# Every second column for the weight loads, and reversed streams, in sixteen column chunks of a two-block transformer kernel

## The chip, the cores and the metric

The kernel runs on one core of a Trainium2 chip. The metric is device time in microseconds (us) of that core. TensorE (PE in the profile) multiplies; VectorE (DVE) and ScalarE (ACT) prepare its operands and take its results away; the DMA queue of SyncE (SPq) brings the weights from HBM. GpSimd does nothing here.

## The reference

Two transformer blocks on one sequence of 256 tokens and 2048 features, in float32. The first block is a gated linear recurrence beside dilated attention. What matters for the change is its input projection `w_in` and what is done with two of its column ranges, `rnn_gate` and `g_rnn`, 2048 columns each:

```python
h = rms_norm(x, ln_pre_g[layer])
proj = jnp.einsum('bsd,de->bse', h, w_in[layer])
rnn_x, rnn_gate, q, k, v, attn_gate, g_rnn, g_attn = split_columns(proj)
hr = rg_lru(rnn_x, ...)                                  # convolution, two gates, a scan over time
y_rnn = jnp.einsum('bsc,cd->bsd', hr * jax.nn.silu(rnn_gate), w_rnn_out[layer])
...                                                      # three groups of dilated attention -> y_attn
merged = jax.nn.sigmoid(g_rnn) * y_rnn + jax.nn.sigmoid(g_attn) * y_attn
y = jnp.einsum('bsd,de->bse', merged, w_o[layer])
x = x + rms_norm(y, ln_post_g[layer])
```

The second block does two layers of three attention branches, each with a wide input projection, a branch projection and an output projection. The change does not touch its arithmetic.

## The kernel before

**Precision.** Every weight and every activation is held as a pair of fp32r numbers, high and low: `hi` is the number copied into fp32r, `lo` is the rest. A product is `hi*hi + hi*lo + lo*hi`. Activations stand transposed, features on the partitions: `hT` (and `uT`) holds for each of 16 feature tiles 512 columns, 256 tokens of `hi` and then 256 of `lo`.

**A unit** is 1024 rows by 256 columns of a weight matrix, 8 row tiles of 128. Its two halves `h` = 0, 1 have 4 row tiles each. The DMA brings a half into `raw` (L390), ScalarE copies it to `hi` in `hl` (L945), VectorE writes `lo = raw - hi` into `hl` (L1288), and TensorE multiplies. `j` (0 or 1) says which half of the 2048 rows of the matrix a unit is and which of the two slots of `hl` it lies in. Two units, `j` = 0 and 1, make a chunk `c` of 256 output columns, in two PSUM banks of `pg` (`s` = 0, 1, 128 columns each).

**A pair** is what TensorE does for one row tile `k` and one bank `s`: a *wide* matmul, with the 128x128 `hi` weights loaded and all 512 columns of `hT` streamed, and a *narrow* one, with the `lo` weights loaded and the 256 columns of `hi` of `hT` streamed into the second half of the bank. So a pair is two weight loads of 128 columns and 768 streamed columns; a half unit is 4 row tiles x 2 banks = 8 pairs, 16 matmuls. The weights of bank `s` are the columns `s*128` to `s*128+127` of the row tile's 256, side by side in `hl`.

**The values of the attention** take the form `token_major`: there the activations are loaded and the weights streamed, `hi` and `lo` in one pattern of 2 x 256. A pair has the same two loads and 768 columns.

**Order.** It is written out by hand in the source. TensorE waits for `lo_done` before each half, and before the first half of a chunk for `evac_done` (its banks are free). `in_order` sets the order of wide and narrow inside a half: wide and narrow in turn, but for the row tiles listed in the table `SIDE`, where the wide ones of both banks come first and then the narrow ones.

**Where the change is.** Stage RG: 16 chunks, of which 0 to 7 are `rnn_gate` and 8 to 15 are `g_rnn`; 16 chunks x 2 units x 2 halves = 64 halves, 512 pairs, all on `hT`. Between chunks TensorE also computes the gates of the recurrence (L716: 64 matmuls of 256 columns on plain fp32 operands of `xres` into `pa`), while ScalarE and VectorE work on the recurrence beside their splitting of weights. The layout of `hl` is used by all stages: `part(j, e, h, a, n)` (L226) gives the place of slot `j`, `hi` or `lo` (`e`), half `h`.

Of the kernel before, what the change touches and what calls it, by code (L numbers as in the profile page):

```python
# [22 lines left out]
P = 128  # L23
S = 256
D = 2048
NT = D // P
UC = 2048
CH = 256
NCH = D // CH
# [6 lines left out]
RNN_X, RNN_G, QKV, D_QKV = 0, 2048, 4096, 3072  # L36
Q1, K1, V1 = QKV, QKV + D_QKV, QKV + 2 * D_QKV
Z1 = QKV + 3 * D_QKV
G_RNN, G_ATT = Z1 + 1024, Z1 + 1024 + D
# [54 lines left out]
def ends(first, last):  # L94

    return frozenset(range(first)) | frozenset(range(8 - last, 8))
# [6 lines left out]
SIDE = {  # L103
    "RX": {4: AGAIN},
    "RG": {3: ends(0, 1), 4: ends(1, 0), 7: ends(0, 1), 8: ends(1, 0), 11: ends(0, 1), 12: ends(1, 0), 15: ends(0, 1),
           16: ends(1, 0), 21: ends(0, 1), 22: AGAIN, 23: ends(0, 1), 24: AGAIN},
    "1": {15: ends(0, 2), 16: ends(1, 0), 17: ends(0, 1), 18: ALL, 19: ends(1, 0), 20: ends(0, 1), 21: ends(1, 1),
          22: ends(2, 0)},
    "B": {4: ends(0, 2), 5: ends(2, 0), 6: ends(0, 2), 7: ends(1, 0), 8: ends(0, 1), 9: ends(2, 2), 10: ALL, 11: ends(6, 0)},
    "C": {4: ends(0, 2), 5: ends(2, 0), 6: ends(0, 2), 7: ends(1, 0), 8: ends(0, 1), 9: ends(2, 2), 10: ends(1, 1),  # L110
          11: ends(4, 0)},
# [25 lines left out]
U_RX, U_RG, U_GR, U_YR, U_P1 = 0, 16, 32, 48, 64  # L137
C_RX, C_RG, C_GR, C_YR, C_P1 = 0, 8, 16, 24, 32
# [17 lines left out]
RAW_CHUNKS, RAW_HEAD = 5, 6  # L156


HI_AT, LO_AT, SLOT, HL = 16, UC + 32, 2 * UC + 128, 4 * UC + 224


PRE_SUMS = [1, 2 + NCH, 4 + 2 * NCH]
# [33 lines left out]
def build(nc, xT, w_in, w_gate, w_rnn, w_att, w_o, w_in2, w_uq, w_ukv, w_br, w_out2,  # L196
          vec1, vec2, blam, consts, tabs, bias_c, outT):
    ctx = ExitStack()
    with ctx:
# [25 lines left out]

        def part(j, e, h, a=0, n=UC // 2):  # L226

            first = j % 2 * SLOT + (LO_AT if e else HI_AT) + h * UC // 2 + a
            return hl[:, first:first + n]

        h3 = hT[:, :].rearrange("p (t n) -> p t n", n=512)
# [5 lines left out]
        pg3 = pg[:, :].rearrange("p (b n) -> p b n", n=512)  # L237
# [71 lines left out]
        block = ctx.enter_context(nc.Block())  # L309
# [232 lines left out]
        def _(pe):  # L542
            def mm(out, lhsT, rhs, start, stop):
                return nc.tensor.matmul(out, lhsT, rhs, start=start, stop=stop, skip_group_check=True)  # L544

            def split_view(j, n):

                return [[part(j, e, k * n // (UC // 2), k * n % (UC // 2), n) for k in range(UC // n)] for e in range(2)]

            def in_order(ks, subs, side, wide, narrow):  # L550

                if RUNS in side and len(ks) == 4 and ks[0] % 8 == 0:
                    for k in ks:
                        for s in range(subs):
                            wide(k, s)
                    for k in ks:
                        for s in range(subs):
                            ins = narrow(k, s)
                    return ins
                for k in ks:  # L560
                    for s in range(subs):
                        wide(k, s)
                        if k % 8 not in side:
                            ins = narrow(k, s)
                    if k % 8 in side:
                        for s in range(subs):
                            ins = narrow(k, s)
                return ins

            def feature_major(b, subs, wh, wl, op, ks, start, stop, base, side):  # L570

                return in_order(
                    ks, subs, side,
                    lambda k, s: mm(pg3[:, b + s, :], wh[k - base][:, s * P:s * P + P], op[:, k, :], start and k == ks[0], False),
                    lambda k, s: mm(pg3[:, b + s, S:], wl[k - base][:, s * P:s * P + P], op[:, k, 0:S], False,
                                    stop and k == ks[-1]))

            def token_major(b, hiw, both, op, ks, start, stop, base, side):

                return in_order(  # L580
                    ks, 2, side,
                    lambda k, s: mm(pg3[:, b + s, :], op[:, k, s * P:s * P + P], both[k - base], start and k == ks[0], False),
                    lambda k, s: mm(pg3[:, b + s, S:], op[:, k, S + s * P:S + s * P + P], hiw[k - base], False,
                                    stop and k == ks[-1]))

            def apart_view(j, n):

                return [[part(j, e, h, 0, n) for h in range(2)] for e in range(2)]

            def both_view(j, n):  # L590
                views = []
                for k in range(UC // n):
                    h, a = k * n // (UC // 2), k * n % (UC // 2)
                    first = j % 2 * SLOT + HI_AT
                    pair = hl[:, first:first + 2 * (LO_AT - HI_AT)].rearrange("p (e n) -> p e n", e=2)
                    views.append(pair[:, :, h * UC // 2 + a:h * UC // 2 + a + n])
                return views

            def opening(u0, c0, tiles_ready, first_parts, weights_parts=None, summed=None):
# [20 lines left out]
            def unit(u, j, c, cj, op, first, last, form="f", subs=2, ready=None, halves=(0, 1), first_parts=None, side=()):  # L620

                base = 0 if first else 8
                if form == "k":
                    base, first, last = 0, True, True
                wh, wl = split_view(j, CH)
                if form == "r":
                    wh, wl = ([[w[h][:, k * P:k * P + P] for k in range(4)] for h in range(2)] for w in apart_view(j, 512))
                for h in halves:
                    pe.wait_ge(lo_done, 2 * u + h + 5)
                    if first and h == 0 and c is not None:  # L630
                        pe.wait_ge(evac_done, c + 1)
                    start, stop = first and h == 0, last and h == 1
                    parts = [range(base + 4 * h, base + 4 * h + 4)] if form != "k" or h == 0 else [(4, 5), (6, 7)]
                    if first_parts is not None and h == 0:
                        parts = first_parts
                    for n, ks in enumerate(parts):
                        if ready is not None:
                            ready(ks)
                        b, begin, end = 2 * (cj % 2), start and n == 0, stop and n == len(parts) - 1
                        if form == "r":  # L640
                            ins = feature_major(b, subs, wh[h], wl[h], op, ks, begin, end, base + 4 * h, side)
                        elif form == "t":
                            ins = token_major(b, wh, both_view(j, CH), op, ks, begin, end, base, side)
                        else:
                            ins = feature_major(b, subs, wh, wl, op, ks, begin, end, base, side)
                    ins.then_inc(half_done, 1)
# [60 lines left out]
            def recurrence_gates(q):  # L707
                pe.wait_ge(rc_conv, q + 1)
                pe.wait_ge(rw_landed, 32 * (q // 2 + 1))
                for k in range(4):  # L710
                    t = 4 * (q % 2) + k
                    if q:
                        pe.wait_ge(rc_sig, 4 * q + k - 3)
                    for j in range(2):
                        w = xres[:, (8 + 4 * j) * S:(12 + 4 * j) * S]
                        ins = nc.tensor.matmul(pa3[:, k, j * S:j * S + S], w[:, t * P:t * P + P], x3[:, t, :],  # L716
                                               start=True, stop=True, skip_group_check=True)
                    ins.then_inc(rc_mm, 1)
# [6 lines left out]
            for c in range(2, NCH):  # L725
                for j in range(2):
                    unit(U_RX + 2 * c + j, j, C_RX + c, c, u3 if c < RAW_CHUNKS else h3, j == 0, j == 1,
                         ready=(lambda ks: h_split(0)(ks[0] // 4)) if c == RAW_CHUNKS else None,
                         side=SIDE["RX"].get(2 * c + j, ()))
            for c in range(2 * NCH):  # L730
                for j in range(2):
                    unit(U_RG + 2 * c + j, j, C_RG + c, c, h3, j == 0, j == 1, side=SIDE["RG"].get(2 * c + j, ()))
                for _, q in rec_pe[c]:
                    recurrence_gates(q)
            product(U_YR, C_YR, u3, lambda q: pe.wait_ge(ru_ready, 1 + q))
# [164 lines left out]
            for l in range(2):  # L900
                ul, cl_ = U_L + l * LU_N, C_L + l * LC_N
                for c in range(8):
# [5 lines left out]
                    for j in range(2):  # L908
                        for halves in ((0,), (1,)):
# [5 lines left out]
                                 side=SIDE["head"][l].get(2 * c + j, ()))  # L915
# [5 lines left out]
                for kind in "ABC":  # L921
                    turns = 2 if kind == "A" else 1
                    with pe.Fori(0, PAIRS // turns) as i:
                        for n in range(turns):
                            p = i * turns + n
# [8 lines left out]
        def _(act):  # L934
# [87 lines left out]

            def recurrence(step, q):
                r, i, _, mq = rec(q)
                if step == "tap":
                    xc = rec(q)[2]
# [933 lines left out]
```

## Time and profile before

| | |
|---|---|
| Median of 2 runs | 3123.56 us (3123.31 to 3123.81) |
| The profiled execution: own time | 3123.54 us |
| its span, first to last instruction | 3121.6 us |
| TensorE busy | 3100.0 us (99%) |
| TensorE weight loads busy (beside the matmuls) | 2732.4 us (88%) |
| VectorE busy | 2129.6 us (68%) |
| ScalarE busy | 1734.3 us (56%) |
| DMA share, mean rate | 59.3% of 16 engines, 183 GB/s |
| Granted TensorE clock, mean | 0.998 of 2.4 GHz |
| Stage RG in the span | 99.06 to 288.84 us |

Busy time of TensorE runs from a matmul's start to its modelled end, and matmuls overlap (a wide one is shown with 391 ns, though the next starts well before). What one costs must be read as the distance from start to start: a stretch divided by the matmuls that start in it. The span is 1.9 us short of the execution's own time; this part is taken as fixed.

### The profile page before, as it was taken

Reading aid. Unit: us, or ns where it says so; the run is one execution under the profiler, and the core shown is the slowest. Engines: PE = TensorE matmul, PEld = TensorE weight load, DVE = VectorE, ACT = ScalarE, POOL = GpSimd, SP = SyncE. Lnnn points to the kernel's source line nnn. Section 1 sums busy time; section 2 is a strip of 40 time slices with the busy share of each in tenths; the row PEclk is TensorE's granted clock in tenths of the full one; section 3 lists DMA queues with packets and bytes.
Section 4 is the critical chain, followed back from the end, with each engine's and each line's share of the span. In section 5 each row is a group of like instructions: output and inputs, shape, how many; then the busy total and the mean of one; then the engine's idle time right before and its main releaser. Section 6 shows DMA issues by size and latency. Waiting matters only on the chain.

```text
span 3121.6 us, 52176 instructions
## 1 busy us (share of the span) xinstructions
PE 3100.0 (99%) x18230; PEld 2732.4 (88%) x18230; DVE 2129.6 (68%) x2741; ACT 1734.3 (56%) x2291; POOL 0.2 (0%) x4
## 2 busy tenths in 40 slices
PE   8999999999999899999999999999999999999999
PEld 7888888888888789888888888888888888888888
DVE  7677575766667687766766656777776676665675
ACT  5685444444445556656565555645665656555563
POOL 0000000000000000000000000000000000000000
PEclk9999999999999999999999999999999999999999
DMA  7656665555556565565556666566556555665555
GB/s 230 197 171 202 200 190 169 187 180 172 179 174 211 174 176 159 158 203 173 177 172 194 189 182 182 183 205 185 159 158 203 173 177 172 194 189 183 181 183 180
DMA packets 569809, 571.67 MB, mean 183 GB/s; under 512 B 26352, under 2 KB 565488, under 8 KB 569712
## 3 DMA queue, kind: packets, MB, share of 16 engines
q1 hardware_dynamic: 569712, 570.42, 59.3%
q8 instruction: 56, 0.92, 0.1%
q14 instruction: 41, 0.34, 0.0%
HBM read 568.25 MB, written 2.10 MB: 183 GB/s over the span
## 4 chain that ended last, share of the span: by engine, by line
PE 98%; DVE 1%; ACT 1%; issue 0%; DMA 0%; SPq 0%; ACTq 0%; DVEq 0%
PE pg L544 92%; PE pa L783 1%; PE pa L800 1%; PE pa L544 1%; PE pa L790 1%; PE pa L759 1%; PE pa L801 1%; PE pa L716 0%; DVE hl L1288 0%; PE pa L890 0%; DMA raw<-w_in 0%; ACT hl L945 0%; DVE uT L1369 0%; DVE xres L1747 0%; PE pa L739 0%
## 5 line engine op out<-in xcount | busy, mean ns | idle before, releaser
L544 PE MATMUL pg<-hT,hl 128*128 128x512 f32 x11456 | 2003.8, 335 | 0.9 <-DVE hl L1288 0.9
L544 PEld LDWEIGHTS pg<-hT,hl 128*128 128x128 f32 x11456 | 1742.6, 188 | 241.8 <-DVE hl L1288 4.6
L1288 DVE TENSOR_TENSOR hl<-raw,hl 128x1024 fp32r<-128x1024 f32 (+1 forms) x1071 | 1255.6, 1209 | 304.5 <-ACT hl L945 296.2
L945 ACT ACTIVATE hl<-raw 128x1024 fp32r<-128x1024 f32 (+1 forms) x1071 | 1085.4, 1044 | 300.9 <-PE pg L544 278.9
L544 PE MATMUL pg<-uT,hl 128*128 128x256 f32 (+1 forms) x3712 | 631.4, 331 | 16.9 <-DVE uT L1369 7.9
L544 PEld LDWEIGHTS pg<-uT,hl 128*128 128x128 f32 x3712 | 555.7, 189 | 88.4 <-issue 14.8
L953 ACT ACTIVATE corr<-pg 128x512 f32<-128x512 f32 x286 | 170.3, 595 | 820.8 <-PE pg L544 820.8
L544 PE MATMUL pg<-hl,hT 128*128 128x256 f32 (+1 forms) x1792 | 318.7, 337 | 0.0
L544 PEld LDWEIGHTS pg<-hl,hT 128*128 128x128 f32 x1792 | 276.3, 188 | 39.7
L1295 DVE TENSOR_TENSOR work<-pg,corr 128x512 f32<-128x512 f32 (+1 forms) x154 | 105.8, 687 | 294.5 <-ACT corr L953 294.0
L1120 ACT ACTIVATE work<-work,sm 128x256 f32<-128x256 f32 (+3 forms) x144 | 69.3, 482 | 130.3 <-DVE sm L1566 128.3
L1295 DVE TENSOR_TENSOR gat<-pg,corr 128x512 f32 (+1 forms) x71 | 49.0, 690 | 134.5 <-ACT corr L953 134.5
L1295 DVE TENSOR_TENSOR xres<-pg,corr 128x512 f32<-128x512 f32 x32 | 22.1, 691 | 42.1 <-ACT corr L953 42.1
L1566 DVE TENSOR_REDUCE sm<-work 128x1 f32<-128x256 f32 (+3 forms) x144 | 49.0, 391 | 1.9
L1126 ACT ACTIVATE uT<-work 128x256 f32 x52 | 20.0, 414 | 53.2 <-DVE work L1697 53.2
L992 ACT ACTIVATE work<-pa,sm 128x256 f32<-128x256 f32 (+1 forms) x58 | 42.1, 725 | 3.7 <-PE pa L701 2.1
L1575 DVE RECIPROCAL sm<-sm 128x2 f32<-128x2 f32 (+1 forms) x56 | 9.5, 169 | 50.3 <-ACT work L1120 50.3
L1562 DVE SCALAR_TENSOR_TENSOR work<-pa,tab 128x384 f32<-128x384 f32 (+2 forms) x56 | 43.6, 779 | 0.0
L800 PE MATMUL pa<-work 128*128 128x256 f32 x144 | 42.8, 379 | 0.0
L993 ACT ACTIVATE work<-work 128x256 f32<-128x256 f32 (+1 forms) x58 | 39.8, 686 | 1.8
L988 ACT ACT_TABLE_LOAD x31 | 39.8, 1283 | 1.3 <-PEq L1954 0.7
L1295 DVE TENSOR_TENSOR corr<-pg,corr 128x512 f32<-128x512 f32 x15 | 10.4, 692 | 44.0 <-ACT corr L953 44.0
(191 smaller groups left out, 1369.3 us busy)
## 6 DMA issues: line engine op xcount, KB each, us to landing
raw<-w_in SPq DMA_DIRECT2D x791, 512.0 KB, 4.7
raw<-w_br SPq DMA_DIRECT2D x96, 512.0 KB, 4.5
raw<-w_out SPq DMA_DIRECT2D x64, 512.0 KB, 4.7
raw<-w_rnn SPq DMA_DIRECT2D x32, 512.0 KB, 4.7
raw<-w_o SPq DMA_DIRECT2D x32, 512.0 KB, 5.2
raw<-w_att SPq DMA_DIRECT2D x16, 512.0 KB, 4.3
raw<-w_uq SPq DMA_DIRECT2D x16, 384.0 KB, 4.0
tab<-tabs SPq DMA_DIRECT2D x5, 896.0 KB, 7.0
```

What stands on the lines that cost most here:

```text
L544: return nc.tensor.matmul(out, lhsT, rhs, start=start, stop=stop, skip_group_check=True)
L800: nc.tensor.matmul(weighted(kind, e), va, pt[:, 0:S], start=m == 0, stop=False, skip_group_check=True)
L945: nc.scalar.activation(part(j, 0, h, 0, n), raw[:, bass.ds(j % 2 * UC + a, n)], ACT.Copy)\
L953: nc.scalar.activation(cr[:, cj % 2, 0:n, :], pg3[:, b:b + n, S:], ACT.Copy)\
L988: act.preload_act_table_set("natural_log_exp_and_others")
L992: steps.done(nc.scalar.activation(out, mean, ACT.Ln, bias=eps, scale=scale))
L993: ins = nc.scalar.activation(out, out, ACT.Exp, scale=-0.5)
L1120: ins = nc.scalar.activation(part, part, ACT.Exp, bias=nmax[:, n:n + 1], accum_out=lsum[:, n:n + 1])
L1288: tt(part(j, 1, h, 0, n), raw[:, bass.ds(j % 2 * UC + a, n)], part(j, 0, h, 0, n).bitcast(F32), ALU.subtract).then_inc(lo_done, 1)
L1295: return tt(out, pg3[:, b:b + n, 0:S], cr[:, cj % 2, 0:n, :], ALU.add)
L1562: steps.done(stt(sc.rearrange("p (m n) -> p m n", m=nm), pa3[:, bank:bank + nm, 0:SM], SCALE[kind], tab[:, m0:m0 + SM * nm].rearrange("p ( ...
L1566: ins = nc.vector.tensor_reduce(nmax[:, n:n + 1], part, AX.XY if kind == "1" else AX.X, ALU.max, negate=True)
```

## The change

The launcher permutes columns of `w_in` before the launch: in the column ranges `rnn_gate` and `g_rnn`, for rows 0 to 1023 and 1536 to 2047, each group of 256 columns is stored so that the columns of bank 0 stand at even places and those of bank 1 at odd ones. Rows 1024 to 1535 (`j` = 1, `h` = 0) keep their order. In stage RG, the new form `p` (`paired_columns`) then loads the 128 columns `s, s+2, s+4, ...` of a row tile, where they were permuted. In the halves (`j`, `h`) = (0, 1) and (1, 0) the moving operand is read from its last column to its first, and the bank is written in the same reversed order. The products and the places of the results are as before.

| half | weight load | stream | halves, pairs |
|---|---|---|---|
| j 0, h 0 | every second column | forward | 16, 128 |
| j 0, h 1 | every second column | backward | 16, 128 |
| j 1, h 0 | side by side | backward | 16, 128 |
| j 1, h 1 | every second column, `hl` 32 numbers further on | forward | 16, 128 |

`hl` grows from 8416 to 8672 numbers per partition. `lo` stands 128 numbers further behind `hi`, slot 1 stands 128 further behind slot 0, and the second half of slot 1 a further 32. `both_view`, which streams `hi` and `lo` together for the values, is written for the new places. Taken by 128 numbers, all places but those of that last half keep their remainder (16 for `hi`, 32 for `lo`), and so does the start of `hT` behind `hl`.

```diff
-HI_AT, LO_AT, SLOT, HL = 16, UC + 32, 2 * UC + 128, 4 * UC + 224
+HI_AT, LO_AT, SLOT, HL = 16, UC + 160, 2 * UC + 256, 4 * UC + 480
+MORE = ((0, 0), (0, 32))
...
-            first = j % 2 * SLOT + (LO_AT if e else HI_AT) + h * UC // 2 + a
+            first = j % 2 * SLOT + (LO_AT if e else HI_AT) + MORE[j % 2][h] + h * UC // 2 + a
...
+            def paired_columns(b, wh, wl, op, ks, start, stop, base, side, strided, backward):
+
+                def weights(w, k, s):
+                    return w[k - base][:, s:2 * P:2] if strided else w[k - base][:, s * P:s * P + P]
+
+                def wide(k, s):
+                    out, x = pg3[:, b + s, :], op[:, k, :]
+                    return mm(out[:, ::-1] if backward else out, weights(wh, k, s), x[:, ::-1] if backward else x,
+                              start and k == ks[0], False)
+
+                def narrow(k, s):
+                    out, x = pg3[:, b + s, S:], op[:, k, 0:S]
+                    return mm(out[:, ::-1] if backward else out, weights(wl, k, s), x[:, ::-1] if backward else x, False,
+                              stop and k == ks[-1])
+
+                return in_order(ks, 2, side, wide, narrow)
...
-                    first = j % 2 * SLOT + HI_AT
+                    first = j % 2 * (SLOT - 80) + HI_AT
                     pair = hl[:, first:first + 2 * (LO_AT - HI_AT)].rearrange("p (e n) -> p e n", e=2)
-                    views.append(pair[:, :, h * UC // 2 + a:h * UC // 2 + a + n])
+                    a += h * UC // 2 + MORE[j % 2][h] + j % 2 * 80
+                    views.append(pair[:, :, a:a + n])
...
+                        elif form == "p":
+                            ins = paired_columns(b, wh, wl, op, ks, begin, end, base, side, (j, h) != (1, 0),
+                                                 (j, h) in ((0, 1), (1, 0)))
...
-                    unit(U_RG + 2 * c + j, j, C_RG + c, c, h3, j == 0, j == 1, side=SIDE["RG"].get(2 * c + j, ()))
+                    unit(U_RG + 2 * c + j, j, C_RG + c, c, h3, j == 0, j == 1, "p", side=SIDE["RG"].get(2 * c + j, ()))
...
+    win = np.array(arrays["w_in"], dtype=f32)
+    for c in (RNN_G, G_RNN):
+        for rows in (slice(0, 1024), slice(1536, 2048)):
+            block = win[rows, c:c + D]
+            win[rows, c:c + D] = block.reshape(-1, NCH, 2, P).transpose(0, 1, 3, 2).reshape(block.shape)
+    arrays["w_in"] = win
```

No engine's instructions are added, left out or moved: in the two programs each engine and the DMA queue have the same rows in the same order, with the same shapes (5991 rows on TensorE, 1564 on VectorE). Only the patterns and places of operands differ.

## Rows read from the trace of the kernel before

**Rows 1.** The page: engines, granted clock by slices, chain by engine, TensorE's three forms.
```profile
PE 3100.0 (99%) x18230; PEld 2732.4 (88%) x18230; DVE 2129.6 (68%) x2741; ACT 1734.3 (56%) x2291; POOL 0.2 (0%) x4
...
PEclk9999999999999999999999999999999999999999
...
PE 98%; DVE 1%; ACT 1%; issue 0%; DMA 0%; SPq 0%; ACTq 0%; DVEq 0%
...
L544 PE MATMUL pg<-hT,hl 128*128 128x512 f32 x11456 | 2003.8, 335 | 0.9 <-DVE hl L1288 0.9
...
L544 PE MATMUL pg<-uT,hl 128*128 128x256 f32 (+1 forms) x3712 | 631.4, 331 | 16.9 <-DVE uT L1369 7.9
...
L544 PE MATMUL pg<-hl,hT 128*128 128x256 f32 (+1 forms) x1792 | 318.7, 337 | 0.0
```

**Rows 2.** Groups by form, stage RG (99.06 to 288.84): matmuls and weight loads.
```profile
L544 PE MATMUL pg<-hT,hl 128*128 128x512 f32 x513 | 173.5, 391 | 0.9 <-DVE hl L1288 0.9
L544 PE MATMUL pg<-hT,hl 128*128 128x256 f32 x513 | 137.6, 276 | 0.0
L716 PE MATMUL pa<-xres 128*128 128x256 f32 x64 | 14.5, 379 | 0.0
...
L544 PEld LDWEIGHTS pg<-hT,hl 128*128 128x128 f32 x1024 | 155.0, 188 | 21.8 <-DVE hl L1288 1.3
```

**Rows 3.** Windows: stage RG, then five halves of it, then four of token_major.
```profile
core 0: us, PE busy (x) PEld busy (x) DVE busy (x) ACT busy (x) POOL busy (x), PEclk, DMA share, GB/s
99.06:288.84 189.78, 188.90 (x1090) 166.59 (x1089) 142.37 (x168) 139.14 (x190) 0.00 (x0) 1.00 0.59 183
101.84:115.44 13.60, 13.60 (x82) 12.03 (x81) 7.62 (x9) 7.36 (x11) 0.00 (x0) 1.00 0.70 218
446.72:457.81 11.09, 11.09 (x66) 9.74 (x65) 8.10 (x11) 4.61 (x5) 0.00 (x0) 1.00 0.60 191
```

**Rows 4.** Windows: nine transposes (L790), plain fp32 matmuls (L716), narrow ones alone.
```profile
476.45:477.32 0.87, 0.87 (x10) 0.87 (x9) 0.00 (x0) 0.59 (x2) 0.00 (x0) 1.00 1.04 350
121.10:123.70 2.60, 2.60 (x14) 2.28 (x13) 2.56 (x3) 2.58 (x4) 0.00 (x0) 1.00 0.56 160
247.05:248.01 0.96, 0.96 (x10) 0.95 (x8) 0.96 (x2) 0.96 (x2) 0.00 (x0) 1.00 0.99 339
```

**Rows 5.** Who waited for whom in stage RG: total, times, longest.
```profile
ACT corr L953 <- PE pg L544: 32.6, 12, 3.7
DVE hl L1288 <- ACT hl L945: 31.1, 23, 5.8
...
ACT hl L945 <- DMA raw<-w_in: 5.1, 4, 2.1
...
PE pg L544 <- DVE hl L1288: 0.9, 2, 0.5
```

**Rows 6.** Timeline around one of the two waits of TensorE in stage RG.
```profile
230.02 1.06 ACT L1066 ACTIVATE work<-gat 128x1024 f32<-128x1024 f32 x1
230.99 1.99 ACT L945 ACTIVATE hl<-raw 128x1024 fp32r<-128x1024 f32 x2
232.06 2.37 DVE L1288 TENSOR_TENSOR hl<-raw,hl 128x1024 fp32r<-128x1024 f32 x2 [1.28 <-ACT hl L945]
...
233.34 9.91 PE L544 MATMUL pg<-hT,hl 128*128 128x512 f32 x56 [0.40 <-DVE hl L1288]
```

## The prediction

> **What bounds the kernel now.** The page comes first [rows 1]: TensorE is busy for 99% of the span, the chain of waits is 98% TensorE, and the clock is granted in full in all 40 slices. So only TensorE's own pace and its waits can move the end. The waits come next, in the stage that the change edits [rows 5]: TensorE waited 0.9 us there in all, twice, out of 189.78 us [rows 3]. The long waits in the same answer are those of ScalarE for TensorE (32.6 us) and of VectorE for ScalarE (31.1 us): the others follow TensorE. What is left is the pace inside a half, and there the busy figures mislead. The group by form gives a wide matmul 391 ns and a narrow one 276 ns [rows 2], which overlap; the pace is the stretch divided by the matmuls that start in it. Five halves of the stage are 80 matmuls, 40 pairs, in 13.60 us (the row counts two more that overlap the edges): 340 ns for a pair [rows 3]. The stage has 64 halves of 8 pairs, 512 pairs (the groups count 513, one from the edge [rows 2]), so 512 x 0.340 = 174.1 us of the stage's 189.8 are pairs at this pace. The rest is the 64 plain fp32 matmuls of the recurrence's gates at 2.60/12 = 217 ns [rows 4], 13.9 us, and 1.8 us of waits and of changes of order. In this stage, then, there is next to nothing to gain outside the pair.
>
> **What a pair could cost.** Two rows bound it. The plain fp32 matmuls of 256 columns start every 217 ns [rows 4]. If these cross the array twice per column (my reading of this row beside the narrow ones), a column costs 0.423 ns and a pair of 768 columns 325 ns. At the full granted clock of 2.4 GHz and one column a cycle, 768 columns are 320 ns. So a pair at 340 ns has 15 to 20 ns in it that its columns don't explain. The weight loads don't fill it either: nine transposes, each with a load of 128 columns, start every 0.87/8 = 109 ns [rows 4], while a pair leaves 170 ns for each of its two loads. That the extra depends on how the two operands are read is shown by the values' form: the same loads and columns, but with loads from hT and streams from hl, take 11.09 us for 32 pairs, 347 ns [rows 3]. And narrow matmuls alone, eight in a row, start every 0.96/8 = 120 ns [rows 4], against 340/3 = 113 for 256 columns of a mixed pair. So patterns and the spacing of loads move a pair by 7 ns or more, with no other engine in the way.
>
> **The change, part by part.**
>
> Host permutation: outside the device time; the DMAs keep shape, size and order. Cost 0.
>
> The new places in hl: ScalarE and VectorE write, and TensorE reads, the same numbers in the same shapes. All places move by multiples of 128 numbers, so each keeps its remainder, except the last half of slot 1 (32 further). If that counted in other stages, it would touch a quarter of all pairs. The trace has no row with this offset; the spread between the two forms (7 ns) bounds it at 2120 pairs x 7 ns = 15 us to either side. (The page has 16,960 matmuls of these forms, 8480 pairs, a quarter of them in such halves [rows 1].) I take 0, because five successive halves run at one pace although their row tiles, slots and banks lie at different distances from hT: distance by 128 or more doesn't show, and I have no row for 32.
>
> Backward streams, 256 pairs: TensorE issues as many columns as before. From below, the whole extra could go, 20 ns, 256 x 0.020 = 5.1 us. From above, a pattern that is served at half the speed costs what the plain fp32 row costs, 217 ns for 256 columns, so 650 for a pair: 256 x (650 - 340) = 79.4 us. I take 0: nothing in the trace reads or writes in descending order, neighbours stay neighbours, and the nearest row (the values' form, with two separate blocks in one stream) differs by 7 ns only, which would be 1.8 us.
>
> Loads of every second column, 384 pairs: a load of 128 side by side takes at most 109 ns [rows 4]. At the same speed per column it is hidden as now. At half the speed it takes 218 ns: under the wide stream (227 ns, two thirds of the pair) it stays hidden, under the narrow one (113 ns) it sticks out by 105 ns: 384 x 0.105 = 40.3 us. From below: a load of every second column passes over 256 columns' places in 109 ns, and the narrow stream passes over 256 columns in 113 ns. Before, the load moved through hl at half the speed at which the stream moved through hT, so that the two met again and again if they share anything in the memory; now they would go in step. If that is what the extra 15 ns of a pair are, a forward pair with such a load loses them. The forward halves with such loads have 256 pairs: 256 x 0.015 = 3.8 us. In the 128 pairs with backward stream and such a load the two run against each other, and in the 128 with a plain load and a backward stream also; I count nothing there.
>
> **The sum.** 3123.5 (the profiled execution, within 0.1 us of the median) - 3.8 = 3119.7 us, and 0.1 of it is taken back at the waits: the one that ends at 233 us [rows 6] comes after ScalarE's steps of the recurrence (a sigmoid, then two copies to hi, then VectorE's lo), which don't get shorter. The wait grows by what TensorE gains while these steps run, about one forward half's 8 x 0.015 = 0.12 us. ScalarE is caught up with TensorE elsewhere in the stage, it waited 32.6 us for it, so the rest of the gain moves through. Forecast 3119.8 us.
>
> **Rivals.**
>
> (a) No change, within 0.8 us: 3123.5 us. The extra belongs to the fp32r stream itself and not to a meeting of two reads. For it: 340.0 ns holds in every undisturbed half of the stage, whatever k, s and j, where meetings should vary with place. Against it: the 347 and 120 ns above. The Trainium skill speaks for this rival ("TensorE: Matmul & The Clock Gate", "Step-by-step: what each phase is for"): the stream and the weight load have a read port each, and loading takes nothing from a running matmul. By that rule, there is nothing to win and the time stays 3123.5; the difference between the two forms is something it doesn't explain.
>
> (b) A small loss, 1 to 15 us: reversed or spread patterns act as the values' form does, 7 ns more in all 512 pairs, 3.6 us: 3127; or the 32-number offset costs in all stages, up to 3138.
>
> (c) Loads at half the speed, exposed under narrow streams: +40.3 us, 3163.8 us. For it: a narrow stream leaves a load only 4 ns of slack. Against it: no row with a strided load.
>
> (d) Backward streams at half the speed: +79.4 us, 3202.9 us, the case on the other side. Place: the 32 halves (0, 1) and (1, 0); price 310 ns a pair; it decides the verdict once a backward pair takes more than 340 + 62.5/256 = 584 ns, and it outweighs my gain from 355 ns on. For it: results go to the bank in descending order, and no row shows that this costs nothing. Against it: each number's neighbour is still next to it. The Trainium skill ("Advanced Engine Details and Errata", "Memory Cachelines") bears on both patterns. It says that PSUM has lines of two fp32 numbers, and that a pattern which isn't contiguous slows matmuls a lot; read strictly, that is this rival. For SBUF it asks for two hits in a line of 16 bytes, which every second fp32 column still gives, so by it (c) doesn't happen. No row of this trace shows either.
>
> **How the numbers follow.** Gain of 0.8 to 10 us: 0.45, the forecast. (a) 0.21, (b) 0.12, (c) 0.08, (d) 0.13 (with both (c) and (d) in it, up to 3243); a gain beyond 10 us, by the offset in other stages, 0.01. The lower end is all 512 pairs losing the full 20 ns, 10.2 us: 3113. The upper end takes in (c): 3164. What is left out is (d) and the last case, 0.14, and some room inside the cases. A change of 2% is 62.5 us, about what a measurement of this kernel can tell from no change for certain. Only (d) is beyond it: slower 0.13, faster 0.01, within 0.86.
>
> **What the changed profile would show.** Right: stage RG shorter by 3 to 4 us, with halves of 2.60 us at (0, 0) and (1, 1) and of 2.72 us at the other two; all other stages as before; loads still 188 ns in the groups; the waits for lo_done in the stage near 1 us. The pace must be read half by half, since each of the four kinds of half has its own pair of patterns. If (a), all four stay at 2.72. If (c), the halves of three kinds become 3.56 us and narrow starts come 218 ns before the next. If (d), two kinds become 5.2 us. If (b) by the offset, all stages' (1, 1) halves change alone. What would make the prediction wrong altogether is a gain from the reversed halves, or a cost in stages that the change touches by addresses alone.

## The result and the profile after

The changed kernel takes 3146.77 us (median of 2 runs, 3146.38 to 3147.15) against 3123.56 us before. The ratio is 1.0076, 95% interval 1.0059 to 1.0093: slower by 23.2 us. That is small, well under 2% of this kernel, but the interval leaves out 1, and the direction is against the forecast (3119.8 us).

The page of the kernel after, its engines, its clock and its chain, the lines that answer to [rows 1]:

```profile
PE 3124.1 (99%) x18230; PEld 2750.0 (87%) x18230; DVE 2129.9 (68%) x2741; ACT 1734.2 (55%) x2291; POOL 0.2 (0%) x4
...
PEclk9999999999999999999999999999999999999999
...
PE 97%; DVE 1%; ACT 1%; DMA 0%; SPq 0%; issue 0%; ACTq 0%; DVEq 0%
```

TensorE is busy 24.1 us longer with the same 18,230 matmuls at the same clock; VectorE and ScalarE are busy as long as before. So the loss is in TensorE's own pace. Where? Windows of the kernel after, for stage RG as a whole (to compare with the first row of [rows 3]) and then for one half of each kind: the plain half (1, 1) just ahead of stage RG, and in the stage (0, 0), (0, 1), (1, 0) and (1, 1). Columns as in [rows 3].

```profile
99.31:294.07 194.76, 194.51 (x1090) 172.18 (x1089) 142.48 (x168) 139.15 (x190) 0.00 (x0) 1.00 0.57 179
...
96.51:99.31 2.80, 2.80 (x18) 2.46 (x17) 2.59 (x10) 0.00 (x0) 0.00 (x0) 1.00 0.07 26
110.56:113.37 2.81, 2.81 (x18) 2.52 (x17) 1.72 (x2) 2.61 (x4) 0.00 (x0) 1.00 0.23 79
102.11:104.94 2.83, 2.83 (x19) 2.52 (x17) 2.33 (x3) 1.06 (x1) 0.00 (x0) 1.00 0.86 254
104.94:107.75 2.81, 2.81 (x18) 2.44 (x17) 1.40 (x2) 1.06 (x1) 0.00 (x0) 1.00 1.03 343
107.75:110.56 2.81, 2.81 (x18) 2.51 (x17) 0.06 (x1) 0.00 (x0) 0.00 (x0) 1.00 0.84 277
```

The stage takes 194.76 us in place of 189.78, 5.0 us more. The span grew by 3145.2 - 3121.6 = 23.6 us, so 18.6 us come from outside the stage, where the change edits nothing but places in `hl`. The second row shows why: a plain half (1, 1), with side-by-side loads and a forward stream, takes 2.80 us. Before, the halves around the stage took 2.72. Of the other three kinds outside the stage, (0, 1) and (1, 0) still take 2.72 us; (0, 0), which follows a half with the offset, takes 2.73 (2732 ns, the 12 ns more in its first two pairs). Inside the stage, all four kinds take 2.81 to 2.83. Other engines are not the cause: the half in the second row ran beside 2.59 us of VectorE's work and a DMA share of 0.07; another plain half with the offset, in run e2 below, beside 0.62 us and 0.63, and it took 2.80 us too.

The groups by form for stage RG, which answer to [rows 2]:

```profile
L545 PE MATMUL pg<-hT,hl 128*128 128x512 f32 x513 | 179.0, 398 | 0.3 <-DVE hl L1310 0.2
L545 PE MATMUL pg<-hT,hl 128*128 128x256 f32 x513 | 140.0, 281 | 0.0
...
L545 PEld LDWEIGHTS pg<-hT,hl 128*128 128x128 f32 x1024 | 160.6, 194 | 21.1 <-DVE hl L1310 0.6
```

A wide matmul grew from 391 to 398 ns, a narrow one from 276 to 281: together 12 ns; from start to start a pair grew by about as much, from 340 to between 351 and 354 ns. Loads of every second column are shown longer, 194 ns as a mean, but nowhere near double.

Who waited for whom in the stage, which answers to [rows 5]:

```profile
ACT corr L975 <- PE pg L545: 38.7, 14, 4.2
DVE hl L1310 <- ACT hl L967: 31.2, 24, 5.8
...
ACT hl L967 <- DMA raw<-w_in: 4.7, 4, 1.9
...
PE pg L545 <- DVE hl L1310: 0.2, 1, 0.2
```

TensorE's waits fell from 0.9 to 0.2 us: what it loses to its own pace it waits less. ScalarE waits 6 us more for it. The timeline at the wait of [rows 6] shows the same: ScalarE's two copies to `hi` and VectorE's `lo` have kept their lengths, and the weight load that waits for them now has 0.22 us of idle time before it. In the kernel before, the load had 0.60 us there (first row; its matmul had the 0.40 of [rows 6]). The other three rows are of the kernel after.

```profile
233.34 9.83 PEld L544 LDWEIGHTS pg<-hT,hl 128*128 128x128 f32 x57 [0.60 <-DVE hl L1288]
...
234.80 1.99 ACT L967 ACTIVATE hl<-raw 128x1024 fp32r<-128x1024 f32 x2
235.88 2.36 DVE L1310 TENSOR_TENSOR hl<-raw,hl 128x1024 fp32r<-128x1024 f32 x2 [1.28 <-ACT hl L967]
237.15 3.83 PEld L545 LDWEIGHTS pg<-hT,hl 128*128 128x128 f32 x22 [0.22 <-DVE hl L1310]
```

### The profile page after: what moved, and what is told of

Its sections match the earlier page's. It is cut to its first block, busy times and chain, and to the rows that moved or that the text cites. A ratio compares the mean times of both kernels' runs of the same rounds, so it can differ in the third digit from the quotient of the medians.

```text
span 3145.2 us, 52176 instructions
## 1 busy us (share of the span) xinstructions
PE 3124.1 (99%) x18230; PEld 2750.0 (87%) x18230; DVE 2129.9 (68%) x2741; ACT 1734.2 (55%) x2291; POOL 0.2 (0%) x4
## 4 chain that ended last, share of the span: by engine, by line
PE 97%; DVE 1%; ACT 1%; DMA 0%; SPq 0%; issue 0%; ACTq 0%; DVEq 0%
PE pg L545 91%; PE pa L805 1%; PE pa L822 1%; PE pa L545 1%; PE pa L812 1%; PE pa L781 1%; PE pa L823 1%; DVE hl L1310 0%; PE pa L738 0%; PE pa L912 0%; DMA raw<-w_o 0%; DMA raw<-w_in 0%; ACT hl L967 0%; SPq L464 0%; DVE uT L1391 0%
```

## The experiments

The theory from the profile after: what a half takes depends on how its loads lie and walk in the memory against the stream beside them, so each of the three edits (offset, strided load, backward stream) costs 80 to 95 ns per half, two of them together up to 111 (the halves (0, 1)), and the offset costs the most in all because it is in every stage. All times of halves below are the distance from the start of a half's first matmul to the start of the next half's, the most frequent value among the undisturbed halves (those with no wait, no matmul of the gates and no other order of wide and narrow matmuls in them); a window shows one of them, rounded to 10 ns. The four kinds stand in the order (0, 0), (0, 1), (1, 0), (1, 1).

### 1. The parts of the change, one at a time

Four kernels on one chip, each timed against the kernel before (3123.42 us, 25 runs, 3121.86 to 3125.22). So a single run, as in parts 2 to 5, is uncertain by nearly 2 us either way; there the times of halves decide.

```diff
 # e1_no_offset: the changed kernel, but
-MORE = ((0, 0), (0, 32))
+MORE = ((0, 0), (0, 0))
```

> The changed kernel with the offset of 32 numbers in the second half of slot 1 taken out; the strided loads and the backward streams of stage RG stay, and lo and slot 1 stay 128 numbers further on. Theory 'offset': the 32 numbers cost about 83 ns in every (1, 1) half of the plain form in all stages, 18 to 19 us in all; without them the time is 3123.5 + 5 = 3128.5 us, and stage RG stays about 5 us longer than before. Rival 'distance': the larger distance between hi and lo or between the slots costs the time; then it stays at 3146 us. Rival 'stage RG slows the rest': 3146 us too.

Measured 3128.57 us (10 runs, 3126.81 to 3129.70), ratio 1.0017 [1.0007, 1.0026]. Windows of stage RG and of a plain half (1, 1) after it:

```profile
99.07:293.79 194.72, 194.47 (x1091) 172.47 (x1089) 142.57 (x168) 139.14 (x190) 0.00 (x0) 1.00 0.58 179
...
301.97:304.69 2.72, 2.72 (x18) 2.41 (x17) 0.22 (x1) 0.00 (x0) 0.00 (x0) 1.00 0.77 206
```

The plain half is back at 2.72 us with `lo` and slot 1 still 128 numbers further on; the stage stays 4.9 us longer. So about 18 of the 23.2 us hang on the offset of 32 numbers, and the distances of 128 cost nothing.

```diff
 # e2_offset_only: the new places in hl, the old form in stage RG
-                    unit(U_RG + 2 * c + j, j, C_RG + c, c, h3, j == 0, j == 1, "p", side=...)
+                    unit(U_RG + 2 * c + j, j, C_RG + c, c, h3, j == 0, j == 1, side=...)
 # and no permuted columns in w_in
```

> The kernel before with only the new places in hl, the 32-number offset among them; no strided load, no backward stream, no permuted columns. Theory 'offset': every (1, 1) half of the plain form takes about 2803 ns in place of 2720, in stage RG too (16 halves, 1.3 us more than the rest of the loss): 3123.5 + 18.6 + 1.3 = 3143.4 us. Rival 'the strided and backward patterns carry the loss': 3123.5 us.

Measured 3142.65 us (4 runs, 3142.07 to 3142.85), ratio 1.0062 [1.0046, 1.0079], 0.8 us under the forecast of the theory. A window of one plain half (1, 1) in stage RG:

```profile
132.57:135.37 2.80, 2.80 (x18) 2.46 (x17) 0.62 (x1) 0.00 (x0) 0.00 (x0) 1.00 0.63 195
```

The offset alone does it. The two runs add up: 5.2 us (e1) and 19.2 us (e2) are 24.4, less the 16 halves (1, 1) of stage RG that pay in both, 16 x 0.08 = 1.3 us: 23.1, against 23.2 measured.

```diff
 # e3_strided_only, no offset
-                            ins = paired_columns(..., (j, h) != (1, 0), (j, h) in ((0, 1), (1, 0)))
+                            ins = paired_columns(..., True, False)
 # e4_backward_only, no offset, columns not permuted
+                            ins = paired_columns(..., False, True)
```

> Stage RG with every second column in all four kinds of half, all streams forward, no 32-number offset. Theory 'relative place': any change of how the load walks against the stream costs some 90 ns per half: halves of 2810 ns, stage RG 5.5 us longer, 3128.8 us. Rival 'only backward streams cost': 3123.5 us, halves 2720 ns. Rival 'loads of every second column at half speed': excluded by the halves after (2813, not 3560 ns).

> Stage RG with all four kinds of half streaming backward, loads side by side as before, no offset. Theory 'relative place': about 2813 ns per half as the (1, 0) halves have after the change, 64 x 0.093 = 6 us, less 0.6 us of waits that shrink: 3129 us. Rival 'only strided loads cost': 3123.5 us.

Measured 3127.32 us for the strided loads (10 runs, ratio 1.0013 [1.0003, 1.0022]) and 3128.25 us for the backward streams (10 runs, ratio 1.0015 [1.0006, 1.0025]). The forecasts were 3128.8 and 3129. The group of weight loads in stage RG, first of the kernel with strided loads, then of that with backward streams:

```profile
L545 PEld LDWEIGHTS pg<-hT,hl 128*128 128x128 f32 x1024 | 162.1, 195 | 18.9 <-DVE hl L1310 0.7
```

```profile
L545 PEld LDWEIGHTS pg<-hT,hl 128*128 128x128 f32 x1024 | 157.3, 188 | 24.4 <-DVE hl L1310 0.7
```

Each costs alone: all halves of the stage take 2800 ns with strided loads (10 ns per pair) and 2813 with backward streams (12 ns). They don't add: the halves (0, 1) of the changed kernel, which have both, take 2825 to 2831. A load of every second column is shown with 195 ns, one side by side with 188.

### 2. The bank's side or the memory's side

In stage RG, halves (0, 0) read backward and write forward, (0, 1) read forward and write backward, (1, 0) both, (1, 1) neither. The first two put the tokens in reversed order; only the times are of use.

```diff
 # e8_in_or_out
-                    return mm(out[:, ::-1] if backward else out, ..., x[:, ::-1] if backward else x, ...)
+                    return mm(out[:, ::-1] if kind in ((0, 1), (1, 0)) else out, ..., x[:, ::-1] if kind in ((0, 0), (1, 0)) else x, ...)
```

> Stage RG with side-by-side loads and without offset; halves (0, 0) read the stream backward but write forward, (0, 1) read forward but write backward, (1, 0) both, (1, 1) neither; so the first two put the tokens in reversed order. Theory 'relative place of load and stream': (0, 0) and (1, 0) take 2813 ns, (0, 1) and (1, 1) 2720 ns. Rival 'the bank's side': (0, 1) and (1, 0) take 2813, (0, 0) 2720.

Windows of one half of each kind, (0, 0) first:

```profile
135.23:138.05 2.82, 2.82 (x19) 2.45 (x18) 1.73 (x2) 2.60 (x4) 0.00 (x0) 1.00 0.63 176
126.96:129.68 2.72, 2.72 (x19) 2.41 (x17) 0.00 (x0) 2.66 (x8) 0.00 (x0) 1.00 0.80 270
129.68:132.49 2.81, 2.81 (x18) 2.44 (x17) 1.91 (x2) 1.82 (x2) 0.00 (x0) 1.00 0.02 5
132.49:135.23 2.74, 2.74 (x18) 2.42 (x17) 0.46 (x1) 0.00 (x0) 0.00 (x0) 1.00 0.72 207
```

Reading backward costs the whole 94 ns of a half, writing backward nothing. The row of (0, 1) that shows this at 2.72 us follows a half in which the wide matmuls come first. Most often a half (0, 1) takes 2739 ns, but so does (1, 1), which writes forward: right behind a half that is read backward, the next one takes 8, 7 and 5 ns more in its first three pairs and then goes at 340. Time of this one run: 3126.21 us, against 3123.49.

### 3. Absolute or relative place

```diff
 # e10_both_moved: the kernel before with
+        pad = sb("pad", 32)
         hl = sb("hl", HL, F32R)
 # e11_stream_moved: the kernel before with
         hl = sb("hl", HL, F32R)
+        pad = sb("pad", 32)
```

> The kernel before with hl, hT, uT and all behind them moved 32 numbers further on in the memory. Theory 'relative place': loads and streams keep their distance, so every half keeps its 2720 ns and the time is 3123.5 us. Rival 'absolute place of the loads or the streams': the halves go to about 2802 ns and the time to some 3190 to 3200 us.

> The kernel before with hT, uT and all behind them moved 32 numbers further on, hl left in place. Theory 'relative place', counted modulo 64 numbers: as if all loads were shifted by 32, every plain half at about 2800 ns; about 850 plain halves by 0.08 us: 3123.5 + 68 = 3190 us. Rival 'absolute place of the loads': 3123.5 us.

One run each: 3124.85 us with both moved, 3187.16 with the streams moved alone, against 3123.49. Two halves (0, 0) and (0, 1) of the stage after RG, first with both moved, then with the streams moved:

```profile
300.44:303.16 2.72, 2.72 (x19) 2.40 (x17) 1.55 (x3) 2.44 (x3) 0.00 (x0) 1.00 0.63 217
303.16:305.88 2.72, 2.72 (x19) 2.41 (x17) 2.72 (x3) 1.12 (x2) 0.00 (x0) 1.00 0.18 24
```

```profile
307.39:310.21 2.82, 2.82 (x18) 2.47 (x17) 1.65 (x3) 2.49 (x3) 0.00 (x0) 1.00 0.52 176
310.21:313.04 2.83, 2.83 (x18) 2.48 (x17) 2.83 (x3) 1.06 (x1) 0.00 (x0) 1.00 0.24 60
```

Loads and streams moved together by 32 numbers keep 2720 ns; the streams moved against the loads cost 80 to 107 ns in every half of all kinds (2800 or 2827). So for this step of 32 numbers what counts is the distance, not the place. With both moved, 6 of the undisturbed halves of stage RG stay at 2800 ns at an unchanged distance, which the theory doesn't say; more on that in part 5.

### 4. A map of the distances

All loads shifted in `hl`, a different shift for each kind of half, the streams left in place. Three kernels: shifts of -16, 48, 16, 64; of 8, 80, 24, 40; and of -4, 48, 16, 32. Stage RG has strided forward loads in the first two and backward streams in the third.

```diff
-MORE = ((0, 0), (0, 32))
+MORE = ((-16, 48), (16, 64))   # e5_places_a
+MORE = ((8, 80), (24, 40))     # e6_places_b
+MORE = ((-4, 48), (16, 32))    # e12_backward_places
```

> A map of places. The four kinds of half are shifted in hl by -16, 48, 16 and 64 numbers (hi and lo together), in all stages; stage RG loads every second column, forward, so the same run has both patterns at four places. Theory 'relative place': what a half takes depends on the place of its loads against the stream, counted modulo some block, so the four kinds differ from each other outside stage RG, some above 2803 ns and some near 2720, and differently inside it; the time lies well above 3123.5, near 3123.5 + 3 x 19 = 3180 if all shifts but one cost as 32 does. Rival 'the old places are the only aligned ones' (any shift costs the same 83 ns): all four at 2803. A strided half under 2720 ns would bring back the step theory of the prediction.

> The second half of the map: shifts of 8, 80, 24 and 40 numbers, otherwise as the first. Theory 'relative place': shifts that keep a multiple of 16 numbers (64 bytes) behave apart from those of 8, 24 and 40 if the blocks are of 64 bytes; the time again near 3180. Rival: all four at 2803. A strided half under 2720 ns would bring back the step theory.

> All four kinds of half shifted in hl, in all stages: -4, 48, 16 and 32 numbers (hi and lo together); stage RG streams backward with side-by-side loads. Theory 'relative place': outside stage RG the halves take as before for 48, 16 and 32 (about 2770, 2781, 2802 ns), and a new value for -4; inside it the backward ones depend on the place too and differ from the 2813 ns at place 0. Rival 'reading backward costs a fixed 93 ns': 2813 ns at all four places, or 93 on top of the forward value. A backward half under 2720 ns would make a kernel that beats both.

One run each: 3157.31, 3175.48 and 3170.98 us (before: 3123.13, 3123.13 and 3123.06). The first came 23 us under its forecast of 3180, because the shifts of -16, 48 and 16 cost 49 to 62 ns a half where it had taken the 82 of the offset of 32. The guess of the second, that multiples of 16 numbers behave apart from 8, 24 and 40, is not borne out (2780 ns at 16 and at 24). The rival that any shift costs the same is out in all three. Four plain halves in a row of the stage after RG, in the first map (shifts -16, 48, 16, 64) and then in the second (8, 80, 24, 40):

```profile
304.89:307.67 2.78, 2.78 (x19) 2.45 (x17) 1.61 (x3) 2.49 (x3) 0.00 (x0) 1.00 0.49 169
307.67:310.44 2.77, 2.77 (x19) 2.44 (x17) 2.77 (x3) 1.06 (x2) 0.00 (x0) 1.00 0.20 62
310.44:313.22 2.78, 2.78 (x19) 2.45 (x17) 1.64 (x2) 1.06 (x1) 0.00 (x0) 1.00 0.94 286
313.22:315.95 2.73, 2.73 (x18) 2.41 (x17) 0.00 (x0) 0.00 (x0) 0.00 (x0) 1.00 1.00 296
```

```profile
306.28:309.07 2.79, 2.79 (x19) 2.44 (x17) 1.61 (x3) 2.49 (x3) 0.00 (x0) 1.00 0.46 155
309.07:311.85 2.78, 2.78 (x19) 2.45 (x17) 2.78 (x3) 1.06 (x1) 0.00 (x0) 1.00 0.18 50
311.85:314.63 2.78, 2.78 (x19) 2.44 (x17) 1.62 (x2) 1.06 (x1) 0.00 (x0) 1.00 0.93 301
314.63:317.44 2.81, 2.81 (x18) 2.44 (x17) 0.00 (x0) 0.00 (x0) 0.00 (x0) 1.00 0.91 297
```

The last row of the second map is a half with VectorE and ScalarE idle (0.00 us): its 2.81 us are TensorE's own, not a contest with the other engines.

All places that the runs show, most frequent ns of a half. A shift of 0 means: counted modulo 64 numbers, `lo` lies where the streams lie and `hi` 16 numbers before them; every shift in this table moves both.

| shift of the loads | side by side, forward | every second column, forward | side by side, backward |
|---|---|---|---|
| 0 (as before) | 2720 | 2800 | 2813 |
| -4 | 2796 | | 2825 |
| 8 | 2787 | 2821 | |
| 16, and 80 | 2779 to 2782, and 2780 | 2819 (or 2833), and 2820 | 2822 |
| 24 | 2780 | 2837 | |
| 32 | 2800 to 2802 (2827 or 2800 with the streams moved) | | 2827 |
| 40 | 2813 | 2822 | |
| 48, and -16 | 2769 to 2772, and 2773 | 2772 (or 2821), and 2786 | 2826 |
| 64 | 2736 | 2797 | |

The first column repeats after 64 numbers (256 bytes): 16 and 80 agree, -16 and 48 agree, and at 64 the middle pairs go at 340 ns; the 16 ns more are in the first two pairs (7 and 5) and the last (4), next to halves at other places. The place before the change is the only one of eight in this block at 340 ns; four numbers beside it cost 76 ns a half. Strided loads have their own map with a best place at 48, 2772 ns (one of two values there): as fast as plain loads at that place, and worse than plain loads at their best; backward streams are at 2813 to 2827 wherever the loads lie. "A fixed cost for reading backward" comes near for them, except that it doesn't come on top of what a place costs forward. In stage RG several places show a second value (the ones with "or"), so the table is a map of what was most frequent between these neighbours, not of one fixed cost for each place.

A last one shifts `hi` and `lo` apart from each other: `lo` by -16 in (0, 0), `lo` by 32 in (0, 1), `hi` by 16 in (1, 0), `hi` by 32 in (1, 1), all forms as in the kernel before.

```diff
 # e9_hi_or_lo
+MORE = (((0, -16), (0, 32)), ((16, 0), (32, 0)))
-            first = ... + MORE[j % 2][h] + h * UC // 2 + a
+            first = ... + MORE[j % 2][h][e] + h * UC // 2 + a
```

> The kernel before with the new spacing, and hi and lo shifted apart from each other: in half (0, 0) lo by -16, in (0, 1) lo by 32, in (1, 0) hi by 16, in (1, 1) hi by 32. Theory 'each load has its own place against the stream that runs beside it': the hi load runs under the narrow stream and the lo load under the wide one, so each of the four costs a part of what the common shift costs (82 ns a half for 32, 61 for 16, 53 for -16), and a shift of one alone could also go below 2720. Rival 'only the hi loads matter, they have the least room': (0, 0) and (0, 1) at 2720, (1, 1) at 2802.

```profile
305.06:307.85 2.79, 2.79 (x18) 2.44 (x17) 1.61 (x3) 2.49 (x3) 0.00 (x0) 1.00 0.45 156
307.85:310.62 2.77, 2.77 (x18) 2.44 (x17) 2.77 (x3) 1.06 (x1) 0.00 (x0) 1.00 0.19 51
310.62:313.41 2.79, 2.79 (x19) 2.46 (x17) 1.63 (x2) 1.06 (x1) 0.00 (x0) 1.00 0.82 264
313.41:316.23 2.82, 2.82 (x18) 2.45 (x17) 0.00 (x0) 0.00 (x0) 0.00 (x0) 1.00 0.97 335
```

2789, 2772, 2783 and 2822 ns (this run: 3172.96 us, before 3122.56). Both loads matter (the rival expected 2720 ns where `lo` alone was moved); the cost is not a sum of parts (`hi` alone by 32 costs 102 ns, both by 32 cost 80). None goes below 2720.

### 5. One of the two reads standing still

Here a load or a stream reads one column over and over, so the two column ranges are computed from other numbers; only the times are of use.

```diff
 # e7_one_number, stage RG, no offset, no strided and no backward pattern
+                    return w[:, 0:1].broadcast_to([P, P]) if kind in ((0, 0), (1, 0)) else w
+                    if kind in ((0, 1), (1, 0)):
+                        x = x[:, 0:1].broadcast_to([P, 512])
```

> Stage RG forward and without offset, with part of the reading taken away, so the two column ranges are computed from other numbers. In halves (0, 0) each load reads one and the same column 128 times, in (0, 1) each stream reads one column 512 or 256 times, in (1, 0) both, (1, 1) is as before. Theory 'two reads meet': with one of the two standing still a pair changes from 340 ns, down towards 325 where nothing meets. Rival 'the extra 15 to 20 ns belong to the fp32r stream': 340 ns (2720 a half) in all four.

Windows of (0, 0) load standing still, (0, 1) stream standing still, (1, 0) both, (1, 1) neither:

```profile
134.75:137.53 2.78, 2.78 (x18) 2.43 (x17) 1.70 (x2) 2.56 (x4) 0.00 (x0) 1.00 0.59 190
126.67:129.31 2.64, 2.64 (x19) 2.42 (x18) 0.00 (x0) 2.58 (x8) 0.00 (x0) 1.00 0.97 323
129.31:131.95 2.64, 2.64 (x19) 2.42 (x18) 1.62 (x2) 1.93 (x2) 0.00 (x0) 1.00 0.07 25
131.95:134.75 2.80, 2.80 (x19) 2.45 (x17) 0.74 (x1) 0.00 (x0) 0.00 (x0) 1.00 0.66 192
```

With the stream standing still a pair takes 330 ns, whatever the load does: 10 ns of the 340 are the price of a stream that walks. With the load standing still, a pair takes 346 to 348 ns, more than at the good distance. So it is not true that a pair gets cheaper as soon as one of the two reads is taken away; the good place of before is better than a load from one place. (This run took 3121.37 us, before 3123.49.)

The untouched halves (1, 1) came out at 2801 or 2741, not 2720, like the six halves of the run with both moved: at the same distance there are two paces that hold themselves, 340 and 350 ns a pair. The kernel before has both too. In one unbroken run of 128 matmuls on hT, with all places at their old remainders, the first row here goes at 350 ns a pair and the second at 340. The next two rows are of the kernel with both moved, in stage RG ahead of the first matmuls of the gates and behind them:

```profile
1155.26:1158.06 2.80, 2.80 (x18) 2.45 (x17) 2.44 (x7) 0.33 (x1) 0.00 (x0) 1.00 0.91 286
1166.15:1168.87 2.72, 2.72 (x18) 2.40 (x17) 2.18 (x2) 1.06 (x1) 0.00 (x0) 1.00 0.78 213
...
113.20:116.00 2.80, 2.80 (x18) 2.45 (x17) 2.25 (x5) 2.80 (x7) 0.00 (x0) 1.00 0.43 123
133.24:135.96 2.72, 2.72 (x18) 2.42 (x17) 0.62 (x1) 0.00 (x0) 0.00 (x0) 1.00 0.66 194
```

Of 5594 plain pairs of the kernel before whose next pair follows at once, 5149 take 340 ns and 133 take 350. Which pace a half has depends on what ran before it: it is handed on from half to half and changes at a break in the sequence. The six slow halves with both moved stand between the start of the stage and its first gate matmuls; with the streams moved, the halves take 2827 ns up to the first gate matmuls, 2800 from there to the wait at 239 us, and 2827 from then on. What at a break chooses the pace is not shown.

## Why the prediction was wrong

**What bounds the kernel, what a pair is made of.** Right. TensorE's pace is all; 340 ns has more in it than its columns (330 with a stream that stands still); patterns and places move it by 10 ns and more. The sum of the stage holds too.

**The new places in hl.** This is the step that failed. The prediction put "I take 0" with a bound of 15 us, and reasoned that distances of 128 numbers don't show. That held, but it said nothing about 32, for which the prediction had "no row", so the term was put at nothing without a reason. The offset cost 19.2 us alone: 10 ns a pair in the quarter of all pairs that have it and 12 ns in the half behind, where the bound was 7 ns from the values' form. It is a cost in stages that the change touches by addresses alone, which the prediction had named as a sign that it would be wrong altogether. The largest term of the change was in the lines that looked like bookkeeping. The values' form depends on the places too: in the kernel after its halves (1, 1) take 2810 ns in place of 2773. That its 347 ns come from its distances is not shown; no place tried brought it under 2773.

**Loads of every second column.** Neither end came. They are not at half speed (195 ns shown against 188), so the 40.3 us didn't come. The gain by "going in step" didn't come either: 2800 ns a half in place of 2600, a loss of 10 ns a pair where a gain of 15 was forecast, and at no place of the map does a strided half fall below 2720. The idea that load and stream take from each other was right in kind (the distance decides, modulo 64 numbers), and wrong in direction: the kernel before already stood at the one good distance of those tried, and no other pattern came down to 340 ns at any place.

**Backward streams.** Taken as 0, they cost 12 ns a pair, on the reading side alone. Rival (d), half the speed, was far off (2813 ns against 5200). The Trainium skill ("Advanced Engine Details and Errata", "Memory Cachelines") says that a pattern in PSUM that isn't contiguous slows matmuls a lot; writing a bank from its last column to its first cost nothing here (2.72 us), so for this pattern the strict reading doesn't hold. For SBUF it grants full speed with two hits in a line; every second column and the reversed stream both have them, and both cost 10 to 12 ns a pair. With its loads 48 numbers further on, a strided half takes at best 2772 ns, what a plain one takes there. So by the measurement, two hits in a line are not enough to keep the pace; the place against the stream decides with them.

**Rivals.** The outcome is of the kind of rival (b), patterns and offset both, but beyond its bound: it ended at 3138, the offset alone came to 3142.7, and the offset with the patterns to 3146.8. Rival (a) took as its ground that 340.0 ns holds whatever the place; it did for the places of the stage, but these differ by multiples of 128 numbers, so they couldn't have shown a distance counted modulo 64. Elsewhere in the kernel before, 133 pairs at 350 ns were a sign against it. It also leaned on the rule of the Trainium skill ("TensorE: Matmul & The Clock Gate", "Step-by-step: what each phase is for") that load and stream have a port each and that loading takes nothing from the running matmul. The two runs with moved streams disagree: the same loads and streams take 340 or 350 to 353 ns a pair by their distance. The range, 3113 to 3164, held the time only because it was drawn up to rival (c), which didn't happen; that was luck.

**The waits.** The sign was right: TensorE's waits in the stage went against its pace, here 0.7 us less wait for a slower pace.

**What stays open.** What in the memory or in TensorE's reading has a period of 64 numbers; why one distance is good; and what chooses between the two paces at one distance. No version of these that computes the right result beats the kernel before: plain loads and forward streams at its places are the best of all that was tried. Strided loads are better at 48 (2772 ns) than at its places (2800), but not as good.

## What to carry to other kernels

Where a kernel is bound by back-to-back matmuls, the place of a buffer is a term of its own: 32 numbers of padding ahead of one quarter of a buffer cost 19 us of 3123, nearly four times what the new patterns beside it cost (5.2 us). Before costing an edit of layout at nothing, take the remainder of every distance between what is loaded and what is streamed (here modulo 64 fp32 numbers), and ask of each that changes which stages use it. Read the pace from start to start over a half or a loop body: the busy time of matmuls that overlap is not their cost (391 and 276 ns for two that take 340 together). And look for stretches in the slower pace before calling a pace the kernel's own.

## What the runs showed of the hardware

- The pace of fp32r pairs (a 512-column and a 256-column matmul with a 128x128 load each) depends on the distance between load and stream modulo 64 numbers: 340 ns at the best of eight places, 346 to 353 at the others; the kernel takes 3124.85 us after moving both by 32 numbers and 3187.16 us after moving the streams alone.
- A stream that reads one column again and again takes 330 ns a pair; a load that does takes 346 to 348.
- Loads of every second fp32 column are shown with 195 ns against 188 and cost 10 ns a pair at shift 0, and at shift 48, in the faster of two values there (2772 ns a half), nothing over plain loads; reading a stream backward costs 12 ns at shift 0, writing a bank backward nothing.
- At one distance two paces exist, 340 and 350 ns: six undisturbed halves of one run kept the slower one, and the kernel before has it in 133 pairs.
